# A decoder trunk of eight layers' halves: the costs from which the engine orders are laid out

## The reference

```
h = x
for i in range(4):
    h = h + mixer[i % 3](rmsnorm(h, norm_mix[i]))      # A, B, C, A
    h = h + channel_mlp(rmsnorm(h, norm_mlp[i]))
out = rmsnorm(h, norm_final)

mixer A: z = gelu(h @ w_in + b_in); u, v = halves of z (3072 each)
         v = layernorm(v); gate = per group and chunk of 128 positions, tril(w_s) @ v + b_s
         (u * gate) @ w_out
mixer B: p = h @ w_in; trailing means of p over 2, 4, 8, 16 positions, less p, by group of 256 channels
         ((pooled @ w_grp + b_grp) * scale) @ w_out
mixer C: a, g = halves of h @ w_in; y = a * sigmoid(g); causal convolution over 31 positions by channel
         silu(layernorm(y)) @ w_out
channel_mlp: square(relu(h @ w1)) @ w2                 # 1024 -> 4096 -> 1024
```

## Time and profile before

| | |
|---|---|
| median of three runs | 3080.59 us |
| profiled execution | 3079.77 us |
| its span, slowest core (core 3) | 3078.2 us |
| spans of the eight cores | 3070.2 to 3078.2 us |
| PE busy | 3019.1 us, 98% |
| DVE busy | 2267.6 us, 74% |
| ACT busy | 1317.5 us, 43% |
| POOL busy | 738.5 us, 24% |
| data moved by DMA | 445.45 MB, mean 145 GB/s |

### The profile page before, as it was taken

One profiled execution on the slowest core, in us unless ns is written; L12 is line 12 of the kernel. 1 busy time (PEld: TensorE's weight loads), 2 busy tenths in 40 slices (PEclk: granted clock), 3 DMA queues, 4 the chain that ended last, 5 costly groups with the idle time before them and its releaser, 6 DMA issues.

```text
span 3078.2 us, 47408 instructions; the slowest of 8 cores (3070.2 to 3078.2 us)
## 1 busy us (share of the span) xinstructions
PE 3019.1 (98%) x15290; PEld 1439.1 (47%) x15290; DVE 2267.6 (74%) x3775; ACT 1317.5 (43%) x2293; POOL 738.5 (24%) x896
## 2 busy tenths in 40 slices
PE   8999999999999999999999999999999999999998
PEld 3444444444444444444576444444444444444444
DVE  7945767678779987877458788877855757577886
ACT  4312433434655354455534634553322333433554
POOL 1111233101414320132551421212212141201221
PEclk9999999999999999999999999999999999999999
DMA  9699997777867367686422477768897988776674
GB/s 167 109 152 165 165 160 126 164 158 156 165 154 130 62 154 158 150 204 150 104 47 77 100 174 172 166 149 165 140 162 131 160 135 143 155 163 142 153 188 114
DMA packets 137585, 445.45 MB, mean 145 GB/s; under 512 B 12032, under 2 KB 15232, under 8 KB 137344
## 3 DMA queue, kind: packets, MB, share of 16 engines
q0 software_dynamic: 102304, 347.38, 64.4%
q1 hardware_dynamic: 35040, 95.04, 8.7%
HBM read 646.07 MB, written 78.64 MB: 235 GB/s over the span
## 4 chain that ended last, share of the span: by engine, by line
PE 93%; DMA 2%; DVE 2%; issue 1%; ACT 1%; POOL 0%; SPq 0%; DVEq 0%; ACTq 0%; POOLq 0%
PE bank L164 93%; DVE xT L164 1%; DMA xT<-x 1%; DMA x_spill<-xT 1%; DMA ring<-b_w_out 0%; DMA ring<-m_w 0%; DVE m_tv L164 0%; DVE bank L164 0%; DVE hT1v L164 0%; DMA ring<-a_w_in 0%; ACT ring L164 0%; ACT sq L164 0%; ACT rs L164 0%; POOL sacc L164 0%; POOL a_smv L164 0%
## 5 line engine op out<-in xcount | busy, mean ns | idle before, releaser
L164 DVE TENSOR_TENSOR xT<-bank,xT 128x512 f32<-128x512 f32 (+2 forms) x972 | 707.3, 745 | 290.5 <-PE bank L164 270.6
L164 PE MATMUL bank<-m_tv,ring 128*128 128x512 bf16 (+2 forms) x3724 | 814.7, 372 | 11.2 <-DVE xT L164 9.3
L164 PEld LDWEIGHTS bank<-m_tv,ring 128*128 128x128 bf16 x3724 | 358.4, 98 | 434.3 <-issue 24.8
L164 ACT ACTIVATE bank<-bank 128x512 f32<-128x512 f32 x496 | 289.4, 587 | 416.1 <-PE bank L164 340.1
L164 POOL DMA_DIRECT2D ring<-m_w x256 | 137.6, 537 | 1242.4 <-PE bank L164 1189.8
L164 ACT ACTIVATE m_tv<-bank 128x512 bf16<-128x512 f32 x511 | 302.2, 598 | 46.7 <-DVE bank L164 11.2
L164 DVE TENSOR_TENSOR m_tv<-m_tv,m_tv 128x512 bf16<-128x512 bf16 x494 | 221.5, 479 | 97.7 <-ACT m_tv L164 94.9
L164 POOL TENSOR_TENSOR sacc<-sacc,sq 128x512 f32<-128x512 f32 (+1 forms) x162 | 212.0, 1309 | 95.4 <-ACT sq L164 64.0
L164 DVE TENSOR_TENSOR ring<-ring 128x512 bf16<-128x512 bf16 (+1 forms) x384 | 199.9, 537 | 26.7 <-DMA ring<-m_w 18.4
L164 ACT ACTIVATE sq<-xT 128x512 f32<-128x512 f32 (+1 forms) x252 | 152.8, 620 | 144.1 <-POOL sacc L164 91.3
L164 PE MATMUL bank<-m_hv,ring 128*128 128x512 bf16 x704 | 174.6, 379 | 2.2 <-issue 0.3
(11 more groups left out here) (242 smaller groups left out, 4186.5 us busy)
## 6 DMA issues: line engine op xcount, KB each, us to landing
ring<-a_w_in POOLq DMA_DIRECT2D x88, 1024.0 KB, 15.2
ring<-m_w POOLq DMA_DIRECT2D x132, 512.0 KB, 7.1
m_pre<-ring SPq DMA_DIRECT2D x124, 512.0 KB, 6.3
ring<-m_pre POOLq DMA_DIRECT2D x124, 512.0 KB, 7.3
ring<-a_w_out POOLq DMA_DIRECT2D x64, 768.0 KB, 8.5
ring<-m_w POOLq DMA_DIRECT2D x124, 384.0 KB, 6.4
xT<-x SPq DMA_DIRECT2D x16, 512.0 KB, 12.8
ring<-b_w_in POOLq DMA_DIRECT2D x8, 1024.0 KB, 18.7
```

The lines of the kernel that those rows point to most:

```text
L164: return lambda e: getattr(e, _method)(*[_r(a) for a in args], **{k: _r(v) for k, v in kwargs.items()})
```

## The change

The cost functions are given smaller fixed parts, and what is taken off is added behind, to the end of the result alone. A DVE operation on 512 float32 columns, for one, kept its engine for 0.155 + 0.533 us in the plan, and its result was there 0.06 us later. Now it keeps the engine for 0.08 + 0.533 us, and the result is there 0.14 us later. ACT goes from 0.19 + n/1250 with 0.06 behind to 0.08 + n/1250 with 0.17 behind, POOL from 0.2 + n/470 to 0.15 + n/480 with 0.12 behind, the bf16 operations from 0.18 + n/1900 to 0.06 + n/1900, and the issue of a load from 0.75 to 0.55. Two DVE operations with three operands are planned as if they had 560 columns. All other numbers of the plan, and all operations, stay.

```
+    TAIL = {"pe": 0.12, "act": 0.17, "dve": 0.14, "pool": 0.12, "sp": 0.06}
...
-                o.end = s + cost + (0.12 if e == "pe" else 0.06)
+                o.end = s + cost + self.TAIL[e]
...
 def c_act(n=512):
-    return 0.19 + n / 1250.0
+    return 0.08 + n / 1250.0
...
 def c_dve(n=512, mode=1):
-    return 0.155 + n / (960.0 * mode)
+    return 0.08 + n / (960.0 * mode)
...
 def c_pool(n=512):
-    return 0.2 + n / 470.0
+    return 0.15 + n / 480.0
...
-                                           max_dma_last_dim=8192), wr=[rs[i]], cost=0.75,
+                                           max_dma_last_dim=8192), wr=[rs[i]], cost=0.55,
...
-                  rd=[xr(kc, tt), rs_r, pv_res], wr=[hr[kc]], cost=c_dve(), port=True, tag="hT")
+                  rd=[xr(kc, tt), rs_r, pv_res], wr=[hr[kc]], cost=c_dve(560), port=True, tag="hT")
...
     def c_fast(n=512):
-        return 0.18 + n / 1900.0
+        return 0.06 + n / 1900.0
```

More of the change, by code:

```diff
@@ L779, in load_raw @@
             last_load[0] = sc.op("pool", I("dma_start", out=t[:, 0:2048], in_=dram[name][l, idx], max_dma_last_dim=8192), wr=[r],
-                                 cost=0.75, dma=key, nbytes=512 * 2048, tag="load", lat=LOAD_LAT)
+                                 cost=0.55, dma=key, nbytes=512 * 2048, tag="load", lat=LOAD_LAT)
             w_ops.append(last_load[0])
@@ L787, in load_pre @@
             sc.op("pool", I("dma_start", out=t[:, 512:2048], in_=dram["m_w%d" % (kind + 1)][l, idx, :, 512:2048], max_dma_last_dim=8192),
-                  wr=[vr[k] for k in QUADS[1:4]], cost=0.75, dma=key, nbytes=512 * 1536, tag="load", lat=LOAD_LAT)
+                  wr=[vr[k] for k in QUADS[1:4]], cost=0.55, dma=key, nbytes=512 * 1536, tag="load", lat=LOAD_LAT)
             sc.op("pool", I("dma_start", out=t[:, 2048:4096], in_=m_pre[kind, idx], max_dma_last_dim=8192), rd=[pre_r[kind][idx]],
-                  wr=[vr[k] for k in QUADS[4:]], cost=0.75, dma=pre_key[slot_of(t)], nbytes=256 * 2048, tag="pre", lat=LOAD_LAT)
+                  wr=[vr[k] for k in QUADS[4:]], cost=0.55, dma=pre_key[slot_of(t)], nbytes=256 * 2048, tag="pre", lat=LOAD_LAT)
             return four(v), vr
@@ L832, in G1 @@
                     sc.op("dve", I("scalar_tensor_tensor", out=bk.v(), in0=bk.v(), scalar=0.0, in1=rst[tt][0],
-                                   op0=ALU.max, op1=ALU.mult), rd=[rst[tt][1]], wr=[bk], cost=c_dve(), tag="relu")
+                                   op0=ALU.max, op1=ALU.mult), rd=[rst[tt][1]], wr=[bk], cost=c_dve(560), tag="relu")
                 else:
@@ L1131, in body @@
                 sc.op("dve", I("memset", brow[:], 0.0), wr=[br_r], cost=1.7, tag="bv")
-                sc.op("pool", I("dma_start", out=brow[0:1, :], in_=dram["a_bv"][ia:ia + 1, :], max_dma_last_dim=8192), wr=[br_r], cost=0.75,
+                sc.op("pool", I("dma_start", out=brow[0:1, :], in_=dram["a_bv"][ia:ia + 1, :], max_dma_last_dim=8192), wr=[br_r], cost=0.55,
                       dma=sc.dma_key("a_brow"), nbytes=4 * AW, tag="bv")
@@ L1159, in body @@
                 sc.op("pool", I("dma_start", out=bvb[:], in_=dram["a_bv"][ia].partition_broadcast(128), max_dma_last_dim=8192),
-                      wr=bv_r, cost=0.75, dma=sc.dma_key(f"a_bv{ia}"), nbytes=128 * 4 * AW, tag="bv")
+                      wr=bv_r, cost=0.55, dma=sc.dma_key(f"a_bv{ia}"), nbytes=128 * 4 * AW, tag="bv")
             def norm_raw(tt):
```

## The result

The changed kernel takes 3108.03 us in the median of 17 runs, the kernel before, run beside it, 3080.98. The ratio is 1.0085, with a 95% interval from 1.0072 to 1.0099. The forecast was 3080.5, with a range up to 3090: the loss lies far outside it. Ratios, and the times of the experiments, are those of executions in which neither die (cores 0 to 3, cores 4 to 7) ran at a lower clock than it otherwise does.

What follows compares the result with a forecast made beforehand. PE's matmuls, busy 98% of the slowest core's span, were taken to bound the kernel. Terms 6.5 - 4.0 + 0 - 3.0 + 0.7 + 0 = +0.2 us gave 3080.0 to 3080.8, stated as 3080.5; range 3070 to 3090.

Steps and rivals of the forecast that it cites:

- First MLP into the mixer: 950 to 985 us: second b_w_out load queues behind a b_w_in piece, so PE's second run starts later; +6.5 us.
- Second MLP into the convolution: 1495 to 1514 us: c_y copies go before c_T_611, shortening PE's wait, with part of the clock regained; -4 us.
- The convolution's norm: 1612 to 1690 us: longer wait for c_z against a vanished ACT-ring wait; 0, bounds -1.5 and +1.5.
- Convolution into its MLP: 1700 to 1770 us: POOL's additions precede weight loads, so PE's waits for acc, rs and mh2v go; -3 us.
- I take 3, since what POOL did not do for the loads it now does late: 1700 to 1770 us: vanished waits give 4 us, 3 taken; next weight load comes later but stays hidden.
- rival (b): 1722 to 1740 us: POOL's additions slow DVE, 1.14 us per instruction, 5.7 for five; chance 0.21, shared with a longer load.
- The rest: The start and the third passage into mixer A: no change, 0, bounds -1 and +1.
- All terms below are therefore differences at five passages: Whole kernel: waits sit between stages, PE runs without gaps inside; no term beyond 6 to 7 us has room.
- End: 3050 to 3078 us: DVE's scalings by rs_63 move before evictions, PE stalls with less behind it; +0.7 us, bounds -1 and +2.
- Range: Whole kernel: 3070 to 3090 us, taking in slower and faster rivals and 2 us beyond for unforeseen waits.
- 3087.9: Whole kernel: time in us if DVE is slowed beside POOL and the load takes its upper bound; slower by 0.24%.
- The clock: Second MLP into the convolution: a shorter stall might return 3.4 us of clock; a third counted, 1.2 us.

## Why the prediction was wrong

*First MLP into the mixer, +6.5: right.* POOL issued the b_w_in piece at 966.1 and the second b_w_out at 967.5, the wait was 8.54 in place of 3.08 and the lag grew by 5.8. What I left out was the clock behind it, 1.1 us (below).

*Second MLP into the convolution, -4.0: right, -4.7.* The wait fell from 2.96 to 0.84, ACT's gate being what c_y then waits for, and the whole of the clock came back, of which I had counted a third (0.51 in the earlier trace rows; the columns are those of the first window above):

```profile
1519.70:1526.60 6.90, 5.71 (x26) 3.69 (x27) 3.38 (x7) 5.74 (x12) 6.75 (x4) 1.00 0.61 114
```

That the sum fits is luck in part: on core 0, whose clock stood at 1.00 in the window of the earlier trace rows, the stretch gave back only 1.2 us.

*The convolution's norm, 0: +1.4, at its bound.* The wait for c_z grew from 2.23 to 2.91, less than the 1.2 to 1.6 us given for it; the ring wait of 1.47 did go, but it lies in the next stretch.

*Convolution into its MLP, -3.0: -1.5, half of it.* Its own part came true: POOL's acc ran at 1743.45, PE took it at 1745.42 with no wait. But the step "I take 3, since what POOL did not do for the loads it now does late" looked only for late loads. What came late were DVE's ring sums and mh2v beside POOL's ten additions and multiplications between 1732 and 1750, and the waits of 2.47, 2.15 and 0.94 took the place of 0.97, 1.21 and 1.8. That is rival (b), its mechanism and its place, but there it took 1.5 us of the gain and not 5.7.

*The rest, the five stretches without a term, 0: +27.9.* This is the step that failed: "All terms below are therefore differences at five passages", with the rest at 0 and bounds of -1 and +1. I had looked at five passages since waits stood there before; a new order makes waits where none had been. Of the +7.0 before the convolution, 3.4 is the wait for mh1v (DVE beside POOL, shown above), and most of the rest is the clock behind the two waits. Of the +9.1 in the middle of the convolution's MLP, 4.39 is the wait for the eviction at 1801.64 and 2.9 the clock behind it (below). This is rival (b) again, some 50 us behind the place at which I priced it. Its price per instruction was right: 1.76 - 0.41 = 1.35 and 1.75 - 0.74 = 1.01, where I had 1.14. I let five be hit; of the fourteen before 1801.64 alone the meetings made 11.5 - 6.6 = 4.9 us, about four. What I held against it, that the eight evictions beside POOL kept their 0.6, was true and beside the point: an eviction was not stretched itself, but it stands *behind* a stretched instruction.

The other stretches hold small waits, whose cause no run takes apart: POOL's acc at 378, 2249, 2380 and 2511, 0.91 each, DVE's xT 1.42 at 823, 1.57 at 2133 and 1.92 at 3005. With POOL's cost set back the waits for acc went, and 5 us with them (1.0085 to 1.0068, intervals that overlap), though a wait of 2.7 us for c_y came back in that order.

*End, +0.7: -0.7, within its bounds.* PE stood 17 matmuls earlier in its order, not 48, and waited 2.88 us in place of 2.92.

*Range.* Rival (b) was priced at one place. The same kind of instruction stands at others: the eight mh1v alone, at 1.14 each, are up to 9.1 us, and 3087.9 + 9.1 = 3097 would have been its upper end, an estimate that is still 11 us short.

*The clock, of which I had counted only the convolution's,* fell behind the three longest new waits, of 8.54, 3.44 and 4.39 us:

```profile
980.00:1000.00 20.00, 13.09 (x76) 5.78 (x77) 11.61 (x22) 10.68 (x20) 1.35 (x5) 0.74 1.03 162
...
1095.00:1115.00 20.00, 16.56 (x71) 7.16 (x71) 12.62 (x18) 13.69 (x26) 8.63 (x8) 0.91 0.34 73
...
1720.00:1800.00 80.00, 71.95 (x330) 31.86 (x328) 72.09 (x106) 54.93 (x97) 44.67 (x40) 1.00 0.63 130
1800.00:1820.00 20.00, 16.68 (x64) 6.84 (x65) 16.68 (x28) 1.57 (x3) 2.42 (x3) 0.83 0.48 110
```

A low clock costs where PE works, not where it waits. The sixteen matmuls of the second fold took 6.41 us, 5.30 before; the 32 of mh1v at 1098.45 took 8.72, and 32 others 7.07 (at 1731.80); the 28 of m_tv at 1802.46 took 9.12, and 28 others 6.21 (at 1829.70). That is 1.1, 1.7 and 2.9 us, 5.7 of the 10.8 by which PE was busy longer. The waits of 2.47 and 2.15 between 1720 and 1800 left the clock at 1.00.

What stays open: which rule would give this planner a good order. Twelve plans with other numbers than the kernel before stand between 0.9989 and 1.0168 of it, with shorter and with longer numbers among the slow ones, and none of them is faster by more than 0.2%.

## What to carry to other kernels

In an in-order queue planned from costs, look at what stands behind each instruction: a two-operand SBUF instruction on DVE beside POOL cost up to 1.35 us more here, and it was often the eviction queued after it that stopped PE. When a table of costs changes, count such meetings in front of evictions in the whole order, not only where waits stood before. Truer numbers for single instructions did not make a faster plan here, nor did a flat price on each of DVE's two-operand instructions (3117.5 us). To see whether contention is the cause, cut the other engine's work and leave the order as it is.

## What the hardware showed that I had not expected

- The stall goes both ways and lasts about as long as the other's work: a DVE sum of 0.41 us took 1.76 beside a POOL addition of 1.27, and a POOL addition took 4.37 beside seven mh0v of DVE that lasted 4.72 together. In the same order, on cores 5, 6 and 7, DVE was the one held, and the seven took 8.77. The Trainium skill ("Trainium Architecture — The Big Picture", section "What this means for kernel authors") calls the pair's port an exclusive lock and not a split of bandwidth; these rows agree.
- A POOL addition that needs the last one's result follows it 0.20 us after its end in the rows shown, so 1.47 from start to start with the 1.27 of one addition, where both plans had 1.34 to 1.35.
- The granted clock fell behind waits of 8.54, 3.44 and 4.39 us and not behind two of 2.47 and 2.15; with PE's wait before the gates at 0.84 us in place of 2.96, it stood at 1.00 in place of 0.51.
